# Window masks added on VectorE, block heads third, values ahead of the turned outputs in a two-block transformer kernel

## What is computed

```
band = (s_idx > t_idx) & (s_idx <= t_idx + WINDOW)
sc = einsum(q, k) * scale ; sc = where(valid, sc, -inf)
m = maximum(max(sc, -1), sink)
pr = exp(sc - m[..., None]) ; den = sum(pr, -1) + exp(sink - m)
o = einsum(pr / den, v)
```

```
q_a, k_a from low-rank cq, ckv (normed, turned by position)     # mla
fox:  softmax(q k^T * scale + decay)                            # "fox"
moba: causal over the own block of 256 = all tokens             # block heads, "moba"
diff: (softmax(q1 k1^T) - lam * softmax(q2 k2^T)) v             # difference heads
o_d = _rms_norm(o_d, diff_sub_norm) * (1.0 - lam_init)
mem:  attention to 256 tokens of a memory, no mask              # "mem"
mixed = concatenate([o_a, o_b, o_c, o_d, o_e]) ; x = x + mixed @ w_o
```

## Time and profile before

| | |
|---|---|
| median of 3 runs | 1483.44 us (1482.12 to 1485.12) |
| profiled execution, its own time | 1476.83 us |
| its span | 1475.3 us |
| mean granted clock of TensorE | 0.992 |
| busy: PE, PEld | 1439.5 us (98%), 1366.9 us (93%) |
| busy: DVE, ACT, POOL | 969.7 us (66%), 771.6 us (52%), 110.2 us (7%) |
| chain that ended last | PE 75%, DVE 14%, ACT 6%, issue 3%, DMA 1% |
| attention of mixer c | about 467 to 531 us |
| attention of mixer 2, layer 0 and layer 1 | about 818 to 925 us, 1170 to 1278 us |

### The profile page before, as it was taken

One profiled execution on the slowest core, in us unless ns is written; L12 is line 12 of the kernel. 1 busy time (PEld: TensorE's weight loads), 2 busy tenths in 40 slices (PEclk: granted clock), 3 DMA queues, 4 the chain that ended last, 5 costly groups with the idle time before them and its releaser, 6 DMA issues.

```text
span 1475.3 us, 26121 instructions
## 1 busy us (share of the span) xinstructions
PE 1439.5 (98%) x10920; PEld 1366.9 (93%) x10920; DVE 969.7 (66%) x1480; ACT 771.6 (52%) x1219; POOL 110.2 (7%) x100
## 2 busy tenths in 40 slices
PE   7999989999999989999999999999999999999999
PEld 6989989999997889999998789999998788999999
DVE  5575667655588567654486855877756675677763
ACT  6744444444476544443366766544445676544442
POOL 0004111100001001110000000011100000011100
PEclk9999989999999999999999999999999999999999
DMA  8532146555464335655554222555565412355553
GB/s 265 167 114 78 67 146 197 186 186 183 160 208 135 115 115 176 194 178 188 184 172 158 98 86 86 172 184 185 172 201 190 151 60 84 119 173 187 181 179 108
DMA packets 186573, 228.20 MB, mean 155 GB/s; under 512 B 5964, under 2 KB 161228, under 8 KB 186456
## 3 DMA queue, kind: packets, MB, share of 16 engines
q1 hardware_dynamic: 185448, 221.75, 46.7%
q0 software_dynamic: 1008, 4.77, 0.9%
HBM read 225.46 MB, written 1.05 MB: 154 GB/s over the span
## 4 chain that ended last, share of the span: by engine, by line
PE 75%; DVE 14%; ACT 6%; issue 3%; DMA 1%; POOL 0%; ACTq 0%; DVEq 0%; SPq 0%; POOLq 0%
PE bank L496 21%; PE bank L498 20%; PE bank L497 20%; DVE weights_low L787 6%; ACT weights_high L685 3%; PE bank L504 3%; PE bank L2106 2%; PE bank L1007 2%; PE bank L2084 2%; DVE cv L3008 2%; DVE cv L3005 1%; ACT S L2183 1%; DVE pad L2995 1%; DVE cv L3014 1%; DMA weights_raw<-in_w_in_ab 1%
## 5 line engine op out<-in xcount | busy, mean ns | idle before, releaser
L787 DVE TENSOR_TENSOR weights_low<-weights_raw,weights_high 128x1024 fp32r<-128x1024 f32 (+2 forms) x421 | 507.0, 1225 | 273.2 <-ACT weights_high L685 273.0
L685 ACT CAST weights_high<-weights_raw 128x1024 fp32r<-128x1024 f32 (+2 forms) x421 | 425.6, 1033 | 260.1 <-PE bank L498 257.2
L496 PE MATMUL bank<-hT_high,weights_high 128*128 128x256 f32 x1640 | 470.8, 287 | 9.6 <-DVE hT_low L863 5.0
L497 PE MATMUL bank<-hT_low,weights_high 128*128 128x256 f32 x1640 | 466.1, 284 | 0.0
L498 PE MATMUL bank<-hT_high,weights_low 128*128 128x256 f32 x1640 | 466.0, 284 | 0.0
L496 PEld LDWEIGHTS bank<-hT_high,weights_high 128*128 128x128 f32 x1640 | 315.9, 193 | 15.0 <-issue 9.2
L497 PEld LDWEIGHTS bank<-hT_low,weights_high 128*128 128x128 f32 x1640 | 316.1, 193 | 0.3
L498 PEld LDWEIGHTS bank<-hT_high,weights_low 128*128 128x128 f32 x1640 | 316.0, 193 | 0.2
L496 PE MATMUL bank<-aT_high,weights_high 128*128 128x256 f32 x864 | 242.1, 280 | 0.1
L497 PE MATMUL bank<-aT_low,weights_high 128*128 128x256 f32 x864 | 241.1, 279 | 0.0
L498 PE MATMUL bank<-aT_high,weights_low 128*128 128x256 f32 x864 | 241.0, 279 | 0.0
(11 more groups left out here) (427 smaller groups left out, 1825.6 us busy)
## 6 DMA issues: line engine op xcount, KB each, us to landing
weights_raw<-in_w_up SPq DMA_DIRECT2D x32, 1024.0 KB, 5.4
weights_raw<-in_w_down SPq DMA_DIRECT2D x32, 1024.0 KB, 5.0
weights_raw<-in_ffn_w_gate SPq DMA_DIRECT2D x22, 1024.0 KB, 5.3
weights_raw<-in_ffn_w_up SPq DMA_DIRECT2D x22, 1024.0 KB, 5.4
weights_raw<-in_w_in SPq DMA_DIRECT2D x20, 1024.0 KB, 5.0
weights_raw<-in_w_in_ab SPq DMA_DIRECT2D x16, 1024.0 KB, 5.9
weights_raw<-in_ffn_w_down SPq DMA_DIRECT2D x16, 1024.0 KB, 5.2
weights_raw<-in_w_o SPq DMA_DIRECT2D x10, 1024.0 KB, 5.0
```

What stands on the lines that cost most here:

```text
L496: k.E.matmul(out, xh, wh, start=first, stop=False)
L497: k.E.matmul(out, xh, wl, start=False, stop=False)
L685: k.A.copy(w.halves(n)[0], w.raw_part(n)).then_inc(*k.s.weight_high(n))
L787: k.V.tensor_tensor(low, w.raw_part(n), high.bitcast(F32), ALU.subtract).then_inc(*k.s.weight_low(n))
```

## The change

- **Mixer c**: the masks of the window are no longer products. Its groups take `mask=` and go the way of the biased group: DVE brings scores times scale plus mask from PSUM into `S`, takes the maxima there, and the sink's minimum is a small operation behind; ACT's exponentials read `S`. The table of masks shrinks from five to three blocks.
- **Mixer 2, both layers**: the groups are now fox, mla, moba, diff, diff, mem. The norms of moba are made where diff's were and the other way round; the root of fox's norm is made together with that of the low-rank vector. P 1 is no longer late. `values_first=True`: PE makes values ahead of `out_turned` (before: behind it); ACT does `PT` copies and the roots of `finish` ahead of casting a turned output (before: behind it); DVE does `finish` ahead of it.
- **Difference norm**: the norm's weight is multiplied in between the mean and the reciprocal, beside ACT's root; the product with the reciprocal writes `mixed`.

```diff
-OUT_2 = [2, 0, 6, 4, 8]
+OUT_2 = [2, 0, 4, 6, 8]
...
-    k.masks = sbuf("masks", [P, 5 * P], F32R)[:, :]
+    k.masks = sbuf("masks", [P, 3 * P], F32R)[:, :]
...
+        self.brought = bias is not None or mask is not None
...
-        masked = g.causal and g.bias is None
+        masked = g.causal and not g.brought
...
-    skewed([(4, out_turned), (3, values), (2, turned), (1, scores), (4, out_products), (5, out_products_late), (0, prepared)], len(a.groups))
+    begin = [(3, values), (4, out_turned)] if a.values_first else [(4, out_turned), (3, values)]
+    skewed(begin + [(2, turned), (1, scores), (4, out_products), (5, out_products_late), (0, prepared)], len(a.groups))
...
-    skewed([(4, out_turned), (2, turned), (3, values), (0, amid), (1, scores), (4, out_products), (0, prepared), (0, next_ready)], len(a.groups))
+    begin = [(2, turned), (3, values), (4, out_turned)] if a.values_first else [(4, out_turned), (2, turned), (3, values)]
+    skewed(begin + [(0, amid), (1, scores), (4, out_products), (0, prepared), (0, next_ready)], len(a.groups))
...
-                V.scalar_tensor_tensor(m.S[:, i, own, c0:c0 + nk], bank, g.scale, g.bias[:, own, c0:c0 + nk], ALU.mult, ALU.subtract
-                                       ).then_inc(*k.banks.read(key))
+                dst = m.S[:, i, own, c0:c0 + nk]
+                if g.bias is not None:
+                    op = V.scalar_tensor_tensor(dst, bank, g.scale, g.bias[:, own, c0:c0 + nk], ALU.mult, ALU.subtract)
+                else:
+                    op = V.scalar_tensor_tensor(dst, bank, g.scale, spread(g.mask[:, c0:c0 + nk], 1, per), ALU.mult, ALU.add)
+                op.then_inc(*k.banks.read(key))
...
+                V.tensor_tensor(x, x, m.minus_sink[:, 4 * n:4 * n + 4], ALU.min).then_inc(*s.row_max((st, n, t)))
...
-                            (out, kv, 2 * kv), window=True, sink=k.row(1, "sinks")[:, kv * 4:kv * 4 + 4], key_block=lambda c: 2))
+                            (out, kv, 2 * kv), mask=k.const("window_neg"), sink=k.row(1, "sinks")[:, kv * 4:kv * 4 + 4], key_block=lambda c: 2))
...
+        Group(4, P, in_pairs, 64 ** -0.5, True, values(C_MOBA + 512), out(2), scaled=True, gains=heads_2(k, l, "moba")),
         Group(4, P, in_fours(0), 32 ** -0.5, True, values(C_DIFF + 512), None, scaled=True, gains=heads_2(k, l, "diff")),
-        Group(4, P, in_fours(1), 32 ** -0.5, True, values(C_DIFF + 512), out(2), scaled=True, shared=True),
-        Group(4, P, in_pairs, 64 ** -0.5, True, values(C_MOBA + 512), out(3), scaled=True, gains=heads_2(k, l, "moba")),
+        Group(4, P, in_fours(1), 32 ** -0.5, True, values(C_DIFF + 512), out(3), scaled=True, shared=True),
...
-    return Attention(("m2", l), m, groups, 2, ("o_2", l), m.out, copies_by_scalar=True, late=(1,))
+    return Attention(("m2", l), m, groups, 2, ("o_2", l), m.out, copies_by_scalar=True, values_first=True)
...
-    roots("cq", 0, 3)
+    squared_columns("fox", C_FOX, 512)
+    roots("cq", 0, 11)
...
     def finish(n):
-        if n == 3:
+        if n == 2:
             roots("memq", SLOT["memq"], 4)
+        elif n == 4:
             scalar_root(k, (st, "sub"), m.st2[:, :, 0:4])
...
-            vector_inverse(k, (st, "memq"), queries)
+            V.scalar_tensor_tensor(m.d1, m.d1, 1.0 - lam_init, spread(row("sub"), 1, NT), ALU.mult, ALU.mult).then_inc(*s.step())
+            gained = s.step.last()
             vector_inverse(k, (st, "sub"), m.st2[:, :, 0:4])
             V.wait_ge(*s.inverse.at((st, "sub")))
+            V.wait_ge(*gained)
             for t in range(NT):
-                x = m.d1[:, t, :].rearrange("p (n d) -> p n d", n=4)
-                last = V.tensor_tensor(x, x, spread(m.st2[:, t, 0:4], 2, 64), ALU.mult)
-            then(last)
-            V.scalar_tensor_tensor(a.groups[3].out[0], m.d1, 1.0 - lam_init, spread(row("sub"), 1, NT), ALU.mult, ALU.mult
-                                   ).then_inc(*s.mixed((st, 3)))
+                last = V.tensor_tensor(per_head(a.groups[4].out[0][:, t, :], 4, 64), per_head(m.d1[:, t, :], 4, 64), spread(m.st2[:, t, 0:4], 2, 64), ALU.mult)
+            last.then_inc(*s.mixed((st, 4)))
```

More of the change, by code:

```diff
@@ L2005, with __init__ @@
 class Attention:
-    def __init__(self, st, m, groups, slots, key, out, copies_by_scalar=False, late=()):
+    def __init__(self, st, m, groups, slots, key, out, copies_by_scalar=False, late=(), values_first=False):
         self.st, self.m, self.groups, self.slots, self.key, self.out, self.copies_by_scalar = st, m, groups, slots, key, out, copies_by_scalar
-        self.late = late
+        self.late, self.values_first = late, values_first
         self.slot = []
@@ L2026, in exps_done @@
         g = self.groups[n]
-        if g.bias is not None:
+        if g.brought:
             return [k.s.exps.at((self.st, n, t))]
@@ L2234, in scores @@
             V.wait_ge(*a.finished(k, n - 2))
-        if g.bias is not None:
-            biased(n)
+        if g.brought:
+            brought(n)
         else:
@@ L2243, in scores, with brought @@
         next(between, None)
-    def biased(n):
+    def brought(n):
         g, i = a.groups[n], n % 2
@@ L2315, in next_ready @@
             work(n + 1)
-    skewed([(4, out_turned), (3, values), (2, turned), (0, amid), (1, scores), (4, out_products), (0, prepared), (0, next_ready)], len(a.groups))
+    begin = [(3, values), (4, out_turned)] if a.values_first else [(4, out_turned), (3, values)]
+    skewed(begin + [(2, turned), (0, amid), (1, scores), (4, out_products), (0, prepared), (0, next_ready)], len(a.groups))
 def vector_scaled(k, dst, bank, rden, signal):
@@ L2558, in prepare @@
         if n == 0:
+            E.wait_ge(*s.masks.at("masks"))
             E.wait_ge(*s.normed.at((l, "fox")))
@@ L2565, in prepare @@
         elif n == 2:
+            E.wait_ge(*s.turned.at((l, "moba", 1)))
+            for mark in projected_to(k, l, 2048):
+                E.wait_ge(*mark)
+        elif n == 3:
             E.wait_ge(*s.turned.at((l, "diff", 1)))
-        elif n == 4:
-            E.wait_ge(*s.turned.at((l, "moba", 1)))
-            for mark in projected_to(k, l, D_IN2):
+            for mark in projected_to(k, l, 2560):
                 E.wait_ge(*mark)
@@ L2864, in amid @@
     def amid(step):
-        if step == 4:
-            normed("moba", m.hp[:, :, C_MOBA:C_MOBA + 512], 8, m.st2[:, :, 12:20], 2 * ROT_M)
-            turned_heads("moba", C_MOBA, 8, 64, ROT_M, ROT_C + ROT_A)
+        if step == 3:
+            scaled(DIFF)
+            turned_heads("diff", C_DIFF, 16, 32, ROT_D, ROT_C + ROT_A + ROT_M)
+        elif step == 4:
             vector_split(k, k.w.first(("in_2", l, 0, 2560)) + 4)
@@ L2890, in finish @@
             V.wait_ge(*s.lam.at((l, "minus")))
-            V.wait_ge(*k.banks.was_read((st, "values", 2)))
+            V.wait_ge(*k.banks.was_read((st, "values", 3)))
             then(V.scalar_tensor_tensor(m.d1, m.d2, m.lm[:, 66:67], m.d1, ALU.mult, ALU.add))
```

64 lines of the change are left out of this document (34 added, 30 removed).

## The result

The changed kernel takes 1498.99 us (median of 4, 1494.48 to 1499.9), the kernel before beside it 1484.28 us (4 runs): a ratio of 1.011, 95% interval 1.009 to 1.0131. Forecast were 1488.2 us and a range up to 1493.5. The sign was right; +4.8 us was forecast, and +14.7 came by the medians.

A forecast was written before the change was run, and what follows sets the result against it. PE was taken as the bound, busy 1439.5 of 1475.3 us. Per layer 8.1 us of new waits less 5.9 gone plus 1.6 clock; two layers +7.6, mixer c -2.8: +4.8, so 1488.2 us, range 1479.0 to 1493.5.

The forecast's parts named there:

- The waits that go: Mixer 2, per layer: PE's waits ahead of scores 2 (1.1 us, clock 1.6) and between scores 4 and 5 (3.2) vanish, 5.9.
- rival 1: Mixer 2: the new waits come but the clock holds, +1.6 us, 1485.0 us; chance 0.17.
- The waits that come: Mixer 2: new PE waits ahead of scores 4, scores 5, values 5 and P 4, 8.1 us per layer.
- A: Mixer 2, ahead of scores 4: PE waits for T 1's bank, behind ACT's copies, table load, root and cast, 3.5 us.
- B: Mixer 2, ahead of scores 5: PE waits for T 2's bank, behind copies, cast and DVE's low part, 2.1 us.
- the end: End of mixer 2: PE waits 1.0 us ahead of values 5 and 1.5 us ahead of P 4.
- The clock: Mixer 2: one stretch at half clock behind the new waits, 1.6 us per layer; none and three kept for the range.
- Mixer c: Mask products removed from four groups save 2.8 us of PE's path; later exponentials are covered by projection panels, costing nothing.
- rival 4: Mixer c: exponentials end over 3.0 us later and the 2.8 us are given back, +7.6, 1491.0 us; chance 0.10.
- The other edits at nothing: Mixer 2's merged root, moved norms and turnings, and the norm's weight: hidden behind other work, costed at nothing.
- Rival 2: Mixer 2: more stretches at half clock, one more per layer +3.2 us, 1491.4 us, two more 1494.6; chance 0.13.
- Rival 3: Mixer 2: ACT casts the turned output in time, new waits only 4.3 us per layer, 1477.4 or 1480.6 us; chance 0.18.

## Why the prediction was wrong

- **What bounds the kernel: right. The waits that go: right in kind, too large in size.** All of the old waits of mixer 2 are gone in both layers. But the 3.2 us between scores 4 and 5 were the length of the stretch less a sum of its work, while rival 1 of the same text counts 2.3 us of idle time there and the list of waits has 2.2. The 0.9 us left over is time that doesn't go with the waits: 1.8 us in two layers, which the sum lacks.
- **The waits that come: right.** A 3.56 (forecast 3.5), B 2.20 (2.1), the end 1.09 and 1.46 (1.0 and 1.5). Four terms summed from other rows of the trace held to a tenth, and the kernels with the cast first and with the root behind moved A to nothing and to 2.05 as the same sum says. The row of the load, with the root 0.01 us behind its end, priced the load rightly. The Trainium skill ("ScalarE: Activation LUTs", What ACT_TABLE_LOAD costs) adds a drain of 1.38 us to a table load; as an estimate from that page A would have been 4.9, and the 3.56 us measured do not agree with it.
- **The clock: the step that failed.** The text said "I take one stretch per layer, 1.6 us". Two things were mis-sized in it. The length: the stretch of the earlier trace rows, the only one of mixer 2, was taken for the size of any, but behind A it lasts 10.24 or 6.83 us in the profiles; in layer 0 it begins while PE still waits (882.95 against 883.30) and ends in the middle of the next panel; one of 10.24 us costs some 4 us, not 1.6. And the number: the waits at the end set it off too, in three of the four layers of the changed kernel's two profiles. In all, 15.2 us in the profiled executions by the kernel with the zeros (11.5 by the ratios), where 3.2 were summed. Why a stretch lasts as long as it does stays open. The trace before held longer stretches in other places, both behind idle time of PE between mixer and feed-forward (windows, columns as in Rows 2):

```profile
199.64:209.88 10.24, 7.15 (x33) 6.89 (x33) 8.34 (x16) 4.16 (x8) 0.00 (x0) 0.50 0.32 96
...
544.39:551.20 6.81, 4.45 (x21) 4.47 (x22) 5.55 (x12) 2.96 (x6) 0.00 (x0) 0.50 0.22 59
```

They belonged into the bounds. Two such stretches per layer at the 4 us that one costs here would have set the upper end at 2 x 2 x 4 us over the 1485.0 us of the sum without clock, 1501. The range was narrower than its own bounds, too: three stretches per layer, which the text means to keep, are its 1494.6, above the 1493.5 of the range.
- **Mixer c: the size was off by 1.1 us.** The sum gave -2.8; -1.7 came. The cover was checked for the exponentials themselves (PT 0 had time, and PE does not wait for `S` there), but not for what is queued behind them: ACT's later high part, DVE's wait for it, and behind that the reading of the bank which scores 2 fill. It was rival 4 in part, by another mechanism.
- **The other edits at nothing: right**, but for a wait of 0.3 us per layer for a weight half near 850 us that the changed order brings.
- **The sum put right**, for the profiled executions: 4.8 + 12.0 for the clock + 1.1 for mixer c + 1.8 for what did not go + 0.6 for that wait + 0.4 for the four waits, 8.3 and not 8.1 per layer = 20.7 us. They differ by 22.7, of which 3.2 stand ahead of the first product between the first mixer and its feed-forward (197.75 against 200.91), before either of the attentions that the change touches; the other 19.5 agree to about a microsecond. The medians differ by less, since the executions of the kernel before hold on average more half clock (some 31 us by their clocks) than its profiled one (25).
- **The rivals.** Rival 1 (clock holds) was made real by the zeros: +4.7 us by the ratio and +3.3 by the medians against its +1.6; 1.1 of mixer c and the 1.8 counted as gone and not gone account for most of the difference. Rival 2 was the right direction with the wrong price per stretch, and no rival had a longer stretch. Rival 3's mechanism, the turned output read in time, is what the kernel with the cast first does, but it is an edit that the change did not make.

## What to carry to other kernels

A wait of PE is priced with the clock behind it: look in the whole trace for the longest stretch at half clock, not at the nearest one. Where a wait is priced as a stretch less the work in it, check the price against PE's idle time there. Where a stage is moved on one engine, move its partner on the engine that frees its bank: here the place of one cast in ACT's order was worth 17.5 us by the ratios, 21 by the medians. And when an engine gets slower work that "is covered", follow its queue one step further, to what stands behind the next wait on it.

## What the runs showed of the hardware

The granted clock fell from 2.4 to 1.2 GHz behind the wait A in every profile that has it unfilled (3.56 us, and 2.05 us with the root behind: six of six layers, though the five unprofiled executions with 2.05 us had less half clock), for 6.8 to 10.2 us; 33 products of zeros per layer kept it at 2.4 in both layers of the profile. The Trainium skill's "TensorE: Matmul & The Clock Gate" (What's actually happening) says that the slow clock is the default and activity releases it; by that the products of zeros have to help, and they do, by 15.2 us in the profiled executions. With fourteen of them, ahead of scores 4 alone, it still fell there once, for 3.4 us. Behind the shorter waits at the end (1.1 and 1.5 us) it fell in 11 of the 14 layers profiled with them, in both layers of the changed kernel's first profile and in one layer of its second. When one wait of a few us costs as much again behind it, and by chance, medians of single kernels move by several us between sets of runs, which the intervals here reflect.
